# Inputs of the recurrence: low rank rows mixed in the attention stage, two constants added by TensorE, ScalarE started from the products

## The reference

```python
z = z + mu_prev * (z_prev - z) + mu_next * (z_next - z)          # token shift, all 1920 columns
r, k, v, zw_f, zw_b, za_f, za_b, zg = split(z)                   # 3 x 512, then 64, 64, 64, 64, 128
kk = k * rw_k_k;  kk = kk * rsqrt(sum_per_head(kk * kk) + 1e-12)
for d, (zw, za) in enumerate(((zw_f, za_f), (zw_b, za_b))):
    w_raw = rw_w0[d] + tanh(zw) @ rw_w2[d]
    decay = exp(-exp(-softplus(-w_raw) - 0.5))                   # its logarithm: -exp(-0.5) * sigmoid(w_raw)
    a = sigmoid(rw_a0[d] + za @ rw_a2[d])
    k_d = k * (1 + (a - 1) * rw_k_a)
bonus = sum_per_head(r * k * rw_r_k) * v
gate = sigmoid(zg) @ rw_g2
```

## Time and profile before

| | |
|---|---|
| time, median of 3 runs | 6358.67 us (6358.47 to 6360.23) |
| time of the profiled execution | 6360.67 us |
| its span, first to last instruction | 6358.8 us |
| TensorE busy | 5276.5 us, 83% |
| VectorE busy | 3789.7 us, 60% |
| ScalarE busy | 1299.4 us, 20% |
| mean granted TensorE clock | 0.926 |
| HBM traffic | 261 GB/s over the span |

### The profile page before, as it was taken

How to read it: one execution, slowest core, us unless ns; L and a number is a source line. 1 busy time by engine, 2 the same in 40 slices (tenths; PEclk the granted TensorE clock), 3 DMA queues, 4 the chain that set the end, 5 groups by cost and what they waited for, 6 DMA issues and landing times. The chain is left out here.

```text
span 6358.8 us, 68926 instructions
## 1 busy us (share of the span) xinstructions
PE 5276.5 (83%) x25836; PEld 2786.5 (44%) x25836; DVE 3789.7 (60%) x8443; ACT 1299.4 (20%) x3116; POOL 1496.5 (24%) x1408
## 2 busy tenths in 40 slices
PE   7998799896987877778789987998968877777777
PEld 3555488453333333333345554884533333333333
DVE  3544566435677777777534445664256777777775
ACT  1022211112222222222111222111022222222221
POOL 0100000002444444444300000000024444444443
PEclk9999899998999899989999998998989999999998
DMA  3112501335999999999831135113359999999998
GB/s 126 67 58 110 215 31 47 147 116 225 420 420 419 406 419 413 417 410 414 356 110 65 58 128 197 40 39 148 115 238 420 420 419 411 418 409 417 410 419 354
DMA packets 325587, 1664.17 MB, mean 262 GB/s; under 512 B 36072, under 2 KB 69096, under 8 KB 159616
## 3 DMA queue, kind: packets, MB, share of 16 engines
q0 software_dynamic: 193504, 1370.70, 52.3%
q1 hardware_dynamic: 131744, 289.00, 12.5%
HBM read 1585.80 MB, written 73.79 MB: 261 GB/s over the span
## 5 line engine op out<-in xcount | busy, mean ns | idle before, releaser
L2008 PE MATMUL psum<-peer_rows,peer_diagonal 128*128 128x512 f32 x5120 | 2512.5, 643 | 703.5 <-ACT peer_diagonal L2052 703.5
L1960 POOL DMA_INDIRECT peer_rows<-in_peer_rows,peer_index x1280 | 1428.8, 1116 | 3361.3 <-PE psum L2008 1737.7
L2151 DVE CUSTOM_DVE_ANT_0 peer_rows<-peer_rows,h_rows 128x1024 f32<-128x1024 f32 x1280 | 1546.7, 1224 | 839.9 <-DMA peer_rows<-in_peer_rows,peer_index 836.8
L2008 PEld LDWEIGHTS psum<-peer_rows,peer_diagonal 128*128 128x128 f32 x5120 | 1020.3, 205 | 2116.2 <-issue 1211.5
L2052 ACT ACTIVATE peer_diagonal<-ident_sb,peer_weight 128x128 f32<-128x128 f32 x1280 | 409.3, 390 | 705.0 <-DVE peer_weight L2123 698.2
L2046 ACT ACTIVATE peer_active<-peer_dots 128x4 f32<-128x4 f32 x320 | 65.7, 205 | 1643.1 <-DVE peer_dots L2151 1643.1
L468 PE MATMUL psum<-in_weights,h_sb 128*128 128x512 f32 (+1 forms) x800 | 309.9, 549 | 0.0
L968 PE MATMUL psum<-h_sb,rw_in_gate_weights 128*128 128x512 f32 (+1 forms) x768 | 232.1, 469 | 84.3 <-ACT y_rw L1003 57.9
L521 DVE SCALAR_TENSOR_TENSOR conv_acc<-conv_in,conv_taps,conv_acc 128x655 f32<-128x655 f32 x240 | 216.4, 901 | 8.5
L468 PEld LDWEIGHTS psum<-in_weights,h_sb 128*128 128x128 f32 x800 | 152.0, 190 | 158.1 <-issue 154.0
L968 PEld LDWEIGHTS psum<-h_sb,rw_in_gate_weights 128*128 128x128 f32 x768 | 133.5, 220 | 187.1 <-issue 94.1
(11 more groups left out here) (345 smaller groups left out, 6167.5 us busy)
## 6 DMA issues: line engine op xcount, KB each, us to landing
rw_out_mod_weights<-in_w_mod SPq DMA_DIRECT2D x16, 2048.0 KB
in_weights<-in_w_in SPq DMA_DIRECT2D x12, 2048.0 KB, 8.5
peer_rows<-in_peer_rows,peer_index POOLq DMA_INDIRECT x1280
modulation_weights<-in_w_mod SPq DMA_DIRECT2D x8, 2048.0 KB
scratch_rw_scratch<-rw_in_direction SPq DMA_DIRECT2D x20, 768.0 KB, 3.6
wkv_own<-scratch_rw_scratch SPq DMA_DIRECT2D x20, 768.0 KB, 6.8
merge_gates<-scratch_gate_scratch SPq DMA_DIRECT2D x16, 960.0 KB
rw_in_gate_weights<-in_w_gate POOLq DMA_DIRECT2D x24, 512.0 KB, 6.0
```

What stands on the lines that cost most here:

```text
L1960: nc.gpsimd.indirect_dma_start(rows[spot][:, :], None, t.dram["peer_rows"], bass.IndirectOffsetOnAxis(ap=index[j % 4][:, k:k + 1], axis=0) ...
L2008: last = nc.tensor.matmul(t.bank[2 * (i % 2) + c], diagonal[k % DIAGONALS][:, :], rows[spot][:, D + c * 512:D + (c + 1) * 512], start=(j = ...
L2151: v.tensor_tensor_reduce(rows[spot][:, 0:D], rows[spot][:, 0:D], h[:, :], 1.0, 0.0, ALU.mult, ALU.add, dots[b][:, k:k + 1]).then_inc(s["do ...
```

## The change

1. The token shift of the low rank columns moves from the start of `rwkv_inputs_stage` to VectorE's stream in `attention_stage`: six parts (three blocks of 128 features by two groups of tokens), ahead of units 9, 12, 15, 18, 21 and 24, three instructions each, in the form own weight times own value plus two neighbours. Its load goes there too, as SyncE's first. The result is a new tensor `t.lora_mixed`; `t.conv_in` is given back after the projection.
2. The constants of decay and rate are added by matmuls of one row (ones by the constant's row) into the same PSUM bank; the rate's products come first. VectorE's L1084 and L1085 go.
3. ScalarE copies the low rank columns of the next tile before the end of a tile, and begins a tile with the sigmoids of rate and decay straight from PSUM, the decay factor and the gate copy, and empties block 2i before the square of kk.
4. The bonus stands between kk and the reductions that need ScalarE: its two multiplies while ScalarE squares, its sum and product while ScalarE takes the root, from a buffer of its own.
5. TensorE does one gate block ahead of the first products instead of two, and three after the last.

```diff
 def attention_stage(nc, t, s, before, layer):
...
+        mu_lora, mu_lora_own = sbuf("mu_lora", 2, 3), sbuf("mu_lora_own", 3)
...
+        LORA_UNITS = [(HEADS + 1 + 3 * n, j, g) for n, (j, g) in enumerate((j, g) for j in range(3) for g in range(2))]
...
         def _(sp):
+            sp.dma_start(mu_lora[:, :, :], t.dram["mu_lora"][layer, :, :, :]).then_inc(s["mu_loaded"], 16)
...
+            def shift_lora(j, g):
+                (lo, m), at = GROUPS[g], LORA_PAD[g]
+                out = t.lora_mixed[:, j, lo:lo + m]
+                shifted.step(nc.vector.tensor_scalar(out, t.lora[:, j, at:at + m], mu_lora_own[:, j:j + 1], None, ALU.mult))
+                for k, begin in enumerate((at - 1, at + 1)):
+                    shifted.step(nc.vector.scalar_tensor_tensor(out=out, in0=t.lora[:, j, begin:begin + m], scalar=mu_lora[:, k, j:j + 1], in1=out,
+                                                                op0=ALU.mult, op1=ALU.add))
+
             bound(0)
             bound(1)
+            dve.wait_ge(s["mu_loaded"], 16)
+            shifted.step(nc.vector.tensor_tensor(mu_lora_own[:, :], mu_lora[:, 0, :], mu_lora[:, 1, :], ALU.add))
+            shifted.step(nc.vector.tensor_scalar(mu_lora_own[:, :], mu_lora_own[:, :], -1.0, 1.0, ALU.mult, ALU.add))
             for u, (i, h) in enumerate(units):
+                for at, j, g in LORA_UNITS:
+                    if u == at:
+                        shift_lora(j, g)
...
 def rwkv_inputs_stage(nc, t, s, before, layer):
...
             def products(i):
                 pe.wait_ge(s["scalar"], SCALAR.after("lora", i))
-                if i:
-                    pe.wait_ge(s["vector"], VECTOR.after("a1", i - 1))
-                for d in range(2):
-                    b = d * HD
-                    nc.tensor.matmul(t.bank[d][:, :], lora_tile[b:b + HD, 0, :], w2[b:b + HD, :], start=True, stop=True)
-                for d in range(2):
-                    b = d * HD
-                    nc.tensor.matmul(t.bank[2 + d][:, :], lora_tile[b:b + HD, 1, :], a2[b:b + HD, :], start=True, stop=True)
+                for first, row, j, low_rank in ((2, A0, 1, a2), (0, W0, 0, w2)):
+                    for d in range(2):
+                        b = d * HD
+                        nc.tensor.matmul(t.bank[first + d][:, :], lora_tile[b:b + HD, j, :], low_rank[b:b + HD, :], start=True, stop=False)
+                        nc.tensor.matmul(t.bank[first + d][:, :], t.ones[0:1, :], rows[0:1, row + d, :], start=False, stop=True)
                 nc.tensor.matmul(t.bank[4][:, :], lora_tile[:, 2, :], g2[:, :], start=True, stop=True).then_inc(s["products"], 1)
 
             gate(0)
-            gate(1)
             pe.wait_ge(s["loaded"], 80)
             for i in range(TILES):
                 products(i)
-                for b in range(2 * i + 2, min(2 * i + 4, GATES_HERE)):
+                for b in range(2 * i + 1, 2 * i + 3):
                     gate(b)
+            gate(GATES_HERE - 1)
...
+            take_lora(0)
             for i in range(TILES):
+                act.wait_ge(s["products"], i + 1)
                 if i:
-                    act.wait_ge(s["products"], i)
-                nc.scalar.copy(lora_tile[:, :, :], lora[:, :, i * P:(i + 1) * P]).then_inc(s["scalar"], 1)
-                act.wait_ge(s["vector"], VECTOR.after("kk", i))
-                nc.scalar.activation(square[:, :], z[:, 3, :], ACT.Square).then_inc(s["scalar"], 1)
-                empty(2 * i)
-                act.wait_ge(s["vector"], VECTOR.after("kk_eps", i))
-                nc.scalar.activation(root[:, :], total[:, :], ACT.Sqrt).then_inc(s["scalar"], 1)
-                empty(2 * i + 1)
-                act.wait_ge(s["products"], i + 1)
+                    act.wait_ge(s["vector"], VECTOR.after("key1", i - 1))
+                for d in range(2):
+                    nc.scalar.activation(a[:, d, :], t.bank[2 + d][:, :], ACT.Sigmoid).then_inc(s["scalar"], 1)
+                for d in range(2):
+                    if i:
+                        act.wait_ge(stores[2 + d], 16 * i)
+                    nc.scalar.activation(per[d][:, 0, :], t.bank[d][:, :], ACT.Sigmoid).then_inc(s["scalar"], 1)
+                for d in range(2):
+                    act.wait_ge(s["scalar"], SCALAR.after(f"decay_sigmoid{d}", i))
+                    nc.scalar.mul(per[d][:, 0, :], per[d][:, 0, :], DECAY_SCALE).then_inc(s["scalar"], 1)
                 if i:
                     act.wait_ge(stores[1], 16 * i)
                 nc.scalar.copy(extra[:, 1, :], t.bank[4][:, :]).then_inc(s["scalar"], 1)
...
+                empty(2 * i)
+                act.wait_ge(s["vector"], VECTOR.after("kk", i))
+                nc.scalar.activation(square[:, :], z[:, 3, :], ACT.Square).then_inc(s["scalar"], 1)
+                act.wait_ge(s["vector"], VECTOR.after("kk_eps", i))
+                nc.scalar.activation(root[:, :], total[:, :], ACT.Sqrt).then_inc(s["scalar"], 1)
+                if i + 1 < TILES:
+                    take_lora(i + 1)
+                empty(2 * i + 1)
             empty(GATES_HERE - 2)
             empty(GATES_HERE - 1)
...
-                done.step(v.tensor_tensor(kk, k, rows[:, K_K, :], ALU.mult))
+                done.mark(v.tensor_tensor(kk, k, rows[:, K_K, :], ALU.mult))
+                done.step(v.tensor_tensor(rk[:, :], r, k, ALU.mult))
+                done.step(v.tensor_tensor(rk[:, :], rk[:, :], rows[:, R_K, :], ALU.mult))
                 dve.wait_ge(s["scalar"], SCALAR.after("kk_square", i))
                 done.step(v.tensor_reduce(total[:, :], heads(square[:, :]), AX, ALU.add))
                 done.step(v.tensor_scalar(total[:, :], total[:, :], KK_EPS, None, ALU.add))
+                done.step(v.tensor_reduce(dot[:, :], heads(rk[:, :]), AX, ALU.add))
+                if repeated:
+                    dve.wait_ge(stores[1], 16 * i)
+                done.step(v.tensor_tensor(heads(extra[:, 0, :]), heads(val), spread(dot[:, :]), ALU.mult))
                 dve.wait_ge(s["scalar"], SCALAR.after("kk_root", i))
...
-                dve.wait_ge(s["products"], i + 1)
                 for d in range(2):
                     if repeated:
                         dve.wait_ge(stores[2 + d], 16 * i)
-                    done.step(v.tensor_tensor(per[d][:, 0, :], t.bank[d][:, :], rows[:, W0 + d, :], ALU.add))
-                    done.step(v.tensor_tensor(a[:, d, :], t.bank[2 + d][:, :], rows[:, A0 + d, :], ALU.add))
                     dve.wait_ge(s["scalar"], SCALAR.after(f"a{d}", i))
```

More of the change, by code:

```diff
@@ L869, in rwkv_inputs_stage @@
 def rwkv_inputs_stage(nc, t, s, before, layer):
-    VECTOR = Marks("kept", "from_prev", "from_next", "shift_sum", "z", "kk", "kk_sum", "kk_eps", "kk_inverse", "kk_done", "rk", "rk_row", "rk_sum", "bonus",
-                   *[f"{n}{d}" for d in range(2) for n in ("w", "a", "removal", "factor", "key")])
-    SCALAR = Marks("lora", "kk_square", "kk_root", "gate", "decay_sigmoid0", "decay0", "a0", "decay_sigmoid1", "decay1", "a1")
+    VECTOR = Marks("own", "from_prev", "from_next", "shift_sum", "z", "kk", "rk", "rk_row", "kk_sum", "kk_eps", "rk_sum", "bonus", "kk_inverse", "kk_done",
+                   *[f"{n}{d}" for d in range(2) for n in ("removal", "factor", "key")])
+    SCALAR = Marks("lora", "a0", "a1", "decay_sigmoid0", "decay_sigmoid1", "decay0", "decay1", "gate", "kk_square", "kk_root")
     W0, A0, K_K, K_A, R_K = 0, 2, 4, 5, 6
@@ L887, in rwkv_inputs_stage @@
         per = [sbuf(f"direction{d}", 3, W) for d in range(2)]
-        square, a = sbuf("square", W), sbuf("a", 2, W)
+        square, rk, a = sbuf("square", W), sbuf("rk", W), sbuf("a", 2, W)
         total, root, inverse, dot = (sbuf(n, HEADS) for n in ("total", "root", "inverse", "dot"))
@@ L1018, in _ @@
                 nc.scalar.copy(extra[:, 1, :], t.bank[4][:, :]).then_inc(s["scalar"], 1)
-                for d in range(2):
-                    act.wait_ge(s["vector"], VECTOR.after(f"w{d}", i))
-                    nc.scalar.activation(per[d][:, 0, :], per[d][:, 0, :], ACT.Sigmoid).then_inc(s["scalar"], 1)
-                    act.wait_ge(s["scalar"], SCALAR.after(f"decay_sigmoid{d}", i))
-                    nc.scalar.mul(per[d][:, 0, :], per[d][:, 0, :], DECAY_SCALE).then_inc(s["scalar"], 1)
-                    act.wait_ge(s["vector"], VECTOR.after(f"a{d}", i))
-                    nc.scalar.activation(a[:, d, :], a[:, d, :], ACT.Sigmoid).then_inc(s["scalar"], 1)
+                empty(2 * i)
[6 more added lines that the diff above has]
+                empty(2 * i + 1)
             empty(GATES_HERE - 2)
@@ L1031, in _ @@
         def _(dve):
-            dve.wait_ge(s["mu_loaded"], 16)
-            done = Steps(dve, s["lora_shifted"])
-            for g, (lo, m) in enumerate(GROUPS):
-                at = LORA_PAD[g]
-                here = t.lora[:, :, at:at + m]
-                for k, near in enumerate((t.lora[:, :, at - 1:at - 1 + m], t.lora[:, :, at + 1:at + 1 + m])):
```

(13 more changed lines are left out.)

14 lines of the change are left out of this document (7 added, 7 removed).

## The result

| | before | after |
|---|---|---|
| median (runs beside one another) | 6359.09 us (6358.47 to 6360.23) | 6407.79 us (6407.39 to 6413.23) |
| ratio | | 1.0073, 95% interval 1.0061 to 1.0086 |
| profiled execution, its span | 6360.67, 6358.8 us | 6413.23, 6411.0 us |
| mean granted TensorE clock | 0.926 | 0.922 |

The account below looks back on a forecast made before the run. A loop of VectorE tile, ScalarE square and emptying, and TensorE gate bounds the inputs stage; uncoupled, TensorE needs 1.9 + 103.2 + 5 x 6.1 = 135.6 us. Saving 25.3 us a layer, 6358.7 - 50.6 = 6308 us, range 6303 to 6314.

Parts of the forecast that it names:

- the term for the constants: Inputs stage, each tile's products on TensorE: with the one-row matmuls they take 6.1 us instead of 2.9.
- the upper bound beside it: Products of a tile if nothing overlaps any more: 16 x 0.43 + 0.96 = 7.8 us.
- rival F: One-row matmuls drop TensorE's clock in each tile's products: 8 us a tile, 80 us, 6388 us; chance 0.04.
- The sum: TensorE from its first gate, inputs stage: 1.9 + 103.2 + 5 x 6.1 = 135.6 us, 25.3 us gained a layer.
- Gate blocks: TensorE's gate blocks, inputs stage: 8.6 us each, twelve 103.2 us, plus 1.9 for the low clock at the start.
- Lora move: Low rank rows mixed beside attention: 11.8 us leave VectorE's start of the inputs stage, counted as a gain of 0.
- Attention: Attention stage: TensorE bounds it, so VectorE's added work of 10 us a layer is covered, cost 0.
- ScalarE a tile ahead: Inputs stage: ScalarE empties the gate bank at most 5.1 us after the products; TensorE asks after 6.9, so never waits.
- C: A new wait of TensorE, for ScalarE's chain or late weights, in the inputs stage: 32 us more, 6340; chance 0.12.
- VectorE's own tile: VectorE's work in a tile of the inputs stage falls from 29.2 to 19 us, below TensorE's period of 23.3.
- E: TensorE isn't uncoupled; ScalarE or VectorE still sets a period near 28 us: 6346 to 6371 us; chance 0.05.
- Rival G: Products: row 0 and the upper half can't share a PSUM bank; 7.0 us a tile, 9 us more, 6317; chance 0.12.

Follow-up runs that it names:

- the run with 128 rows: Changed kernel, same matmul order, but each constant's matmul uses all 128 rows (identity times the broadcast row): 6347.53 us, ratio 0.9976.
- the picked row: Changed kernel with constants grouped on 64 rows of each half, stationary tile one in rows 0 and 64, zero elsewhere: 6298.5 us, ratio 0.9901.

## Why the prediction was wrong

**The step that failed** is the term for the constants: "The lower half then has 12 passes, the upper 4: 12 x 0.43 + 0.96 for the gate product = 6.1 us." It measured 14.2, and even the upper bound beside it, 7.8 for "nothing overlaps any more", was far too low. Two assumptions went into both numbers.

*That a pass of one row costs what its neighbours cost, and overlaps as they do.* I took 0.43 us from passes of one shape in a row. Where matmuls of 64 rows alternate one by one with ones of 1, 32 or 128, a matmul of two passes takes 1.05 us and nothing lies beside it. Eight of them and the gate product are 9.2 us (the run with 128 rows): 3.1 above the forecast, 15.5 us a layer. As an estimate from the prediction's own bound, 7.8 - 6.1 = 1.7 of the 3.1 are the overlap, and 1.4 the longer pitch, which no term of the sum had. The Trainium skill, "TensorEngine Tiling (Array Packing)", Key Properties, says that a change of the tiling mode (rows of 32, 64 or 128), as against a change of the tile, drains TensorE. The pitches here agree: two passes, or four side by side, take 0.86 us between neighbours of the same row count, 0.96 with another count on one side and 1.05 on both, so a change costs about 0.19 us, an estimate. The groups of 0.96 us in the kernel before, each with such a change on one side, fit this. I weighed another rule of that page and missed this one.

*That the clock stays up.* This was rival F, at 4%. Its place was right, and its condition: the products alone cost 14.2 - 6.1 = 8.1 us a tile more, over the 5.1 at which it decides. That its price of 8 us is so near is luck: the clock took 14.2 - 9.2 = 5.0 in the products and 0.6 to 1.7 in the passes behind them, 6.1 on average, since it fell only 3 to 5 us into each tile's products; the other 3.1 are the longer and serial matmuls, which F didn't have. What I held against it was a stretch at clock 1.00 with such matmuls in it. A closer look at that stretch, in the timeline of TensorE of the kernel before, shows how thin this was:

```profile
29.25 1.01 PE L157 MATMUL psum<-modulation_bias,ones_sb 1*2 1x512 f32 x2
```

One matmul of 1.0 us among ones of 128 rows. It bears on one small matmul, not on eight in a row, half of them small.

**The sum, with what it measured.** TensorE from its first gate to its last: forecast 135.6 us, measured 182.7. Products 5 x 14.2 instead of 5 x 6.1, 40.4 more: 15.5 for the longer and serial matmuls, 25 for the clock. Gate blocks 111.8 instead of 105.1; of these 6.7 us, 2.4 are in the undisturbed run with the picked row too (130.5 - 5 x 4.6 = 107.5), so my blocks and their slow start were a little too short. The other 4.3 are, but for rounding, 5.5 for the clock behind the products, less 1.3 for a first block that came to the full clock sooner (10.6 us instead of 11.9). 47.1 more than forecast less 25.3 forecast as gain is 21.8 a layer, as measured (21.7).

**The other steps held**, each by its own row. Lora move: 0 (VectorE begins its first tile at 597.58 instead of 597.73, since it waits for its load; undone, nothing changes). Attention: covered. ScalarE a tile ahead: chain of 4.5 us where at most 5.1 was said, no wait of TensorE (C did not occur; the emptying was late only where the products are 2.9, by at most 3.6 us a layer). VectorE's own tile: 19.2, forecast 19; for ScalarE it stands only before the reduction (2.0 to 2.6 us a tile with 64 rows, where 4 were said, because TensorE's period came out at 22.0). E was excluded by this too. With products of 4.6 the sum gives 25.3 + 5 x 1.5 = 32.8 a layer; TensorE ended 30.4 earlier with the picked row, 61 us in both layers, and 63 by the ratio (0.0099 x 6358.7). So the rest of the sum was sound, within 2.4 us a layer.

Rival G (a row tile and its neighbour can't share a bank) was not told apart: where the row counts differ nothing overlaps anyway, and where they agree the two halves never had the same bank.

## What to carry to other kernels

Read the shape of every matmul in a sequence: a small one between larger ones is priced neither by its rows nor by its neighbours' pitch. If a term must be added by TensorE, give it the rows, and the halves, of the matmuls around it, with zeros in the stationary tile for what isn't needed. And where a rival needs a behaviour that the trace shows only in passing, ask how long that passage was before holding it against the rival.

## What the hardware showed that I had not expected

- TensorE's granted clock fell from 1.00 to the level of 0.50 while the engine was never idle, in the products with matmuls of one row (14.2 us a tile) and just so with 32 rows (13.2 to 14.7 us), both beside ones of 64. With 64 rows throughout in the whole change (4.6 to 4.7 us), and with 128 beside 64 (9.2 us), no pass of the products was slow. Whether this goes by the number of rows or by the size of the row tile, the runs don't tell apart.
- A stationary tile with zeros in 63 of 64 rows ran like a full one: products of 4.6 us and a mean clock of 0.98 from first to last block, with 64 equal rows 4.6 us and 0.99.
- Two one-row matmuls on rows 0 and 64 run side by side, as two of 64 rows do; one at a time on row 0 the clock fell in eight tiles of ten, two at a time, at the very end of the products, in three of ten.
- A change of the row count costs TensorE about 0.19 us (an estimate: 1.05 us a matmul with a change before and behind it, 0.86 without), and matmuls of unlike row count don't run side by side even on different halves: a constant on row 0 and the next product on the upper half start 1.05 us apart (632.86 and 633.91 in the kernel after).
